# Splitting the scaled input of a three-pass float32 kernel straight from x, with x loaded in four transfers on ScalarE's queue

## The chip, the cores and the metric

The kernel runs on one core of a Trainium2 chip. The metric is the device time of one execution in microseconds (us), lower is better. The time before is the median of three runs.

## The reference, cut to what matters

Two blocks run one after the other on 256 tokens of width 1024. The first has two layers of: a gated feed-forward net of width 2816, a mixer (sliding-window attention beside a short convolution), and a second feed-forward net. Each of the six begins with an RMS norm, and a seventh norm ends the block. The second block adds 16 meta tokens and does latent attention and 2-D neighbourhood attention once.

```python
def rms_norm(x, gain):
    xf = x.astype(jnp.float32)
    inv = lax.rsqrt(jnp.mean(xf * xf, axis=-1, keepdims=True) + NORM_EPS)
    return (xf * inv).astype(x.dtype) * gain

def swiglu(h, w_gate, w_up, w_down):
    return (jax.nn.silu(h @ w_gate) * (h @ w_up)) @ w_down
...
    for l in range(DEPTH):
        x = x + 0.5 * swiglu(rms_norm(x, ffn1_norm[l]), ffn1_wg[l], ffn1_wu[l], ffn1_wd[l])
        h = rms_norm(x, mix_norm[l])
        z = h @ w_in[l]
...
        x = x + jnp.concatenate([attn_out, conv_out], axis=-1) @ w_out[l]
        x = x + 0.5 * swiglu(rms_norm(x, ffn2_norm[l]), ffn2_wg[l], ffn2_wu[l], ffn2_wd[l])
    return rms_norm(x, final_norm)
```

## The kernel before, in words

Everything is kept feature-major: `x` is a tile of 128 partitions by 8 column tiles (k = 0 to 7) by 256 tokens. Weights come from HBM in pieces, most of them 128x1024 (512 KB: eight 128x128 tiles that make one output tile of 128 features), those of the down projections 128x1408. The pieces go through four slots (`w_raw`). SyncE issues their loads (L286); a slot is loaded again once its low part is done. ScalarE writes the high part of a piece (`w_hi`, L388, in a rounded float32 format), VectorE writes the low part (`w_lo = w_raw - w_hi`, L654), and TensorE multiplies three times per weight tile (`product`, L1043 to L1045): high by high, high by low, low by high.

The input of a matmul is split in the same way into `h_hi` and `h_lo`. For the six norms inside the layers (called q = 0 to 5 here; q = 6 is the norm that ends the first block) the factor of each token is applied after the matmul, so only the norm's weight per feature has to be applied before it. That is done per column tile k in three steps:

- `scaled` (L667, VectorE): `h32 = x * weight`, the weight being one number per partition out of `sml`;
- `high` (L418, ScalarE): `hhi = h32`, rounded;
- `low` (L673, VectorE): `hlo = h32 - hhi`.

Beside it ScalarE squares x (`square`, L400) into one of two buffers `sq`, GpSimd adds the squares of k = 0 to 6 up (`add_squares`: a copy, L331, then six adds, L334), and TensorE sums that and the square of k = 7 over the partitions (`sum_norm`, L1075 and L1077). ScalarE makes the token factors of it (`rstd`, L403 and L405).

Places where these steps stand:

- **The start** (L526 to L535 on ScalarE, L847 to L857 on VectorE): x comes in two transfers of 512 KB (four k each) at the head of SyncE's queue (L281), `sml` in one on ScalarE's queue (L383). Each engine walks over the k in turn, and three splits of weight pieces stand in between.
- **The down projections** `down` (L446 and L715): 16 pieces, two per output tile; after every second piece VectorE updates x (L729), then comes the input split of that k for the next norm.
- **`wout`** (L509 and L836): eight pieces, one per k, x updated at L839.

TensorE meets the new input in `first_pair`: it runs piece 0 over k = 0 to 6, waiting for each `h_lo`, then `sum_norm`, then piece 1 over k = 0 to 6, and only then k = 7 of both:

```python
for k in (*range(KT - 1), KT - 1):
    for o in range(2) if k == KT - 1 else (0,):
        if k == 0:
            ready(0)
        pe.wait_ge(h_lo, q * KT + k + 1)
        mm = product(bank[o][:, 0:T], o, k, *hcols(k), k == 0, k == KT - 1)
...
    if k == KT - 2:
        ready(1)
        sum_norm(q)
        for k1 in range(KT - 1):
            product(bank[1][:, 0:T], 1, k1, *hcols(k1), k1 == 0, False)
```

After the second layer q = 6 takes its sum at once (`sum_norm(6)`) and TensorE has nothing else to do there; `h_hi` and `h_lo` of q = 6 are written and not used, since that norm and the next are computed in another way (`norm`). The two layers are one hardware loop on every engine.

Of the kernel before, what the change touches and what calls it, by code (L numbers as in the profile page):

```python
# [20 lines left out]
F32 = mybir.dt.float32  # L21
# [7 lines left out]
KT = D // P  # L29
# [105 lines left out]
def build(nc, xT, metaT, w8, wd, small, mats, btab, rope, colmask, metabias, relbias, out):  # L135
    with ExitStack() as ctx:
# [73 lines left out]
        x_loaded = [sem(f"x_loaded{p}") for p in range(2)]  # L210
# [65 lines left out]
        def _(sp):  # L276
            for s in raw_full:
                sp.sem_inc(s, 16 * PRIME)
            for p in range(2):
                half = slice(p * KT // 2, (p + 1) * KT // 2)  # L280
                sp.dma_start(x[:, half, 0:T], xT[:, half]).then_inc(x_loaded[p], 16)  # L281

# [37 lines left out]
        def _(pool):  # L320
# [17 lines left out]
            pool.wait_ge(h32_done, KT)  # L338
# [41 lines left out]
        def _(act):  # L380
            for s in (*hi_ready, *silu_done, pt_done):
                act.sem_inc(s, PRIME)
            act.dma_start(sml[:], small).then_inc(g_loaded, 16)  # L383
# [23 lines left out]
            def norm(q, n=T):  # L407
# [3 lines left out]
                for k in range(KT):  # L411
                    act.wait_ge(h32_done, q * KT + k + 1)
                    act.activation(hhi[:, k * TM:k * TM + n], h32[:, k % 4, 0:n], ACT.Copy).then_inc(h_hi, 1)

            def high(q, k, slot):

                act.wait_ge(h32_done, q * KT + k + 1)
                act.activation(hhi[:, bass.ds(k * TM, T)], h32[:, slot, 0:T], ACT.Copy).then_inc(h_hi, 1)  # L418
# [27 lines left out]
            def down(name, nxt, l, q):  # L446
# [5 lines left out]
                def lap(j, last):  # L452
                    for r in range(SLOTS):
                        i = r if not last else DN - SLOTS + r
                        split_ahead(name, nxt, l, i, j, last)
                        if r % 2:
                            p, o2 = r // 2, j if not last else KT // 2 - 1
                            act.wait_ge(acc_step, q * 7 + o2 * 2 + p - 1)
                            act.wait_ge(x_ready[p], q * 4 + o2 + (PRIME - 3))
                            square(p, x[:, o2 * 2 + p, 0:T])  # L460
                            high(q, o2 * 2 + p, p)
# [50 lines left out]
            def wout(l, q):  # L512
                for o in range(KT):
# [5 lines left out]
                    else:  # L519
                        act.wait_ge(acc_step, q * 7 + o - 1)  # L520
                    square(o % 2, x[:, o, 0:T])
                    high(q, o, o % 2)
# [3 lines left out]
            act.preload_act_table_set("natural_log_exp_and_others")  # L526
            for k in range(KT):
                act.wait_ge(x_loaded[k // (KT // 2)], 16)
                if k >= 2:
                    act.wait_ge(acc_step, k - 1)  # L530
                square(k % 2, x[:, k, 0:T])
                high(0, k, k % 4)
                if k in (3, 5, 7):
                    split((k - 3) // 2, PT8, uses0(1))
# [114 lines left out]
        def _(dve):  # L649
# [957 lines left out]
```

## Time and profile before

| | before |
|---|---|
| median of three runs | 1320.96 us (1319.97 to 1323.59) |
| span of the profiled execution | 1319.6 us |
| TensorE matmuls busy | 1287.5 us, 98% |
| VectorE busy | 844.0 us, 64% |
| ScalarE busy | 662.2 us, 50% |
| GpSimd busy | 127.6 us, 10% |

The span is the profiled execution's own time as the profiler sees it; it is 1.4 us below the median of the three runs. A busy share is of the whole span; the change touches a few stretches only, so these shares say which engine sets the pace in general, and the stretches have to be read one by one.

### The profile page before, as it was taken

How to read it: one execution, taken by the hardware profiler on the slowest of the kernel's cores; microseconds unless marked ns; L12 is line 12 of the kernel's file. 1: busy time of each engine (PE TensorE's matmuls, PEld its weight loads, DVE VectorE, ACT ScalarE, POOL GpSimd, SP SyncE). 2: the span in 40 equal slices, each digit the busy share in tenths (PEclk: the TensorE clock that was granted, in tenths of full speed). 3: DMA queues.
4: the chain of work that ended last, by engine and by line, in shares of the span. 5: the costliest groups of instructions: out<-in, count | busy, mean ns of one | idle time of the engine just before them, and what ended most of it. 6: DMA issues, size and time to landing. Idle time of an engine off the chain costs nothing.

```text
span 1319.6 us, 27677 instructions
## 1 busy us (share of the span) xinstructions
PE 1287.5 (98%) x10106; PEld 1220.6 (93%) x10106; DVE 844.0 (64%) x1478; ACT 662.2 (50%) x1153; POOL 127.6 (10%) x149
## 2 busy tenths in 40 slices
PE   6999999999999999999999999999889999999998
PEld 6999999999999999999999999999878769978778
DVE  6676656777667547666558676676566645456565
ACT  5554544555555445445436464554456556434443
POOL 3000000440000000000003510000110000002210
PEclk9999999999999999999999999999989999999999
DMA  7555744345556536557444465566433204433332
GB/s 278 191 188 192 230 153 156 126 144 193 184 188 226 189 103 202 191 186 239 163 133 139 136 195 182 189 212 212 133 109 128 97 1 134 138 132 96 110 99 65
DMA packets 55689, 209.87 MB, mean 159 GB/s; under 512 B 6417, under 2 KB 8465, under 8 KB 55489
## 3 DMA queue, kind: packets, MB, share of 16 engines
q1 hardware_dynamic: 54048, 203.45, 47.0%
q0 software_dynamic: 1424, 5.42, 1.4%
q8 instruction: 43, 0.70, 0.2%
q14 instruction: 30, 0.24, 0.1%
q10 hardware_dynamic: 144, 0.06, 0.0%
HBM read 207.86 MB, written 1.05 MB: 158 GB/s over the span
## 4 chain that ended last, share of the span: by engine, by line
PE 93%; DVE 4%; issue 1%; ACT 1%; DMA 0%; DVEq 0%; ACTq 0%; SPq 0%
PE bank L1043 26%; PE bank L1044 26%; PE bank L1045 25%; PE bank L1081 2%; PE bank L1390 2%; DVE w_lo L654 1%; PE bank L1355 1%; DVE h_lo L673 1%; PE bank L1344 1%; PE bank L1353 1%; PE bank L1354 1%; PE bank L1281 1%; PE bank L1386 1%; PE bank L1283 1%; PE bank L1282 1%
## 5 line engine op out<-in xcount | busy, mean ns | idle before, releaser
L1043 PE MATMUL bank<-h_hi,w_hi 128*128 128x256 f32 (+1 forms) x1992 | 568.6, 285 | 17.6 <-DVE w_lo L654 11.8
L1044 PE MATMUL bank<-h_lo,w_hi 128*128 128x256 f32 (+1 forms) x1992 | 564.4, 283 | 0.0
L1045 PE MATMUL bank<-h_hi,w_lo 128*128 128x256 f32 (+1 forms) x1992 | 559.5, 281 | 0.0
L654 DVE TENSOR_TENSOR w_lo<-w_raw,w_hi 128x1024 fp32r<-128x1024 f32 (+1 forms) x360 | 465.5, 1295 | 81.1 <-ACT w_hi L388 79.7
L388 ACT ACTIVATE w_hi<-w_raw 128x1024 fp32r<-128x1024 f32 (+1 forms) x360 | 397.3, 1107 | 92.7 <-PE bank L1045 69.7
L1043 PEld LDWEIGHTS bank<-h_hi,w_hi 128*128 128x128 f32 x1992 | 377.7, 190 | 30.5 <-issue 26.0
L1044 PEld LDWEIGHTS bank<-h_lo,w_hi 128*128 128x128 f32 x1992 | 376.9, 189 | 0.8
L1045 PEld LDWEIGHTS bank<-h_hi,w_lo 128*128 128x128 f32 x1992 | 377.4, 189 | 0.0
L1043 PE MATMUL bank<-g_hi,w_hi 128*128 128x256 f32 x832 | 232.7, 280 | 0.4 <-DVE x_res L839 0.3
L1044 PE MATMUL bank<-g_lo,w_hi 128*128 128x256 f32 x832 | 232.3, 279 | 0.0
L1045 PE MATMUL bank<-g_hi,w_lo 128*128 128x256 f32 x832 | 232.2, 279 | 0.0
L1043 PEld LDWEIGHTS bank<-g_hi,w_hi 128*128 128x128 f32 x832 | 156.4, 188 | 1.2 <-DVE x_res L839 0.7
L1044 PEld LDWEIGHTS bank<-g_lo,w_hi 128*128 128x128 f32 x832 | 156.4, 188 | 0.0
L1045 PEld LDWEIGHTS bank<-g_hi,w_lo 128*128 128x128 f32 x832 | 156.4, 188 | 0.0
L440 ACT ACTIVATE g_hi<-gated 128x256 f32 (+1 forms) x88 | 37.0, 421 | 166.3 <-DVE gated L709 166.3
L705 DVE TENSOR_TENSOR gated<-bank,rstd 128x256 f32<-128x256 f32 x88 | 37.3, 424 | 95.7 <-PE bank L1045 95.4
L400 ACT ACTIVATE squares<-x_res 128x256 f32<-128x256 f32 (+2 forms) x64 | 26.4, 417 | 126.0 <-DVE x_res L729 101.3
L701 DVE TENSOR_TENSOR squares<-bank,rstd 128x256 f32<-128x256 f32 x88 | 37.4, 425 | 46.9 <-PE bank L1045 46.9
L436 ACT ACTIVATE silu_gate<-squares 128x256 f32<-128x256 f32 x88 | 36.8, 418 | 58.0 <-DVE squares L701 58.0
L334 POOL TENSOR_TENSOR ln_mean<-ln_mean,squares 128x256 f32<-128x256 f32 (+1 forms) x45 | 44.5, 990 | 189.1 <-ACT squares L400 188.7
L331 POOL COPY ln_mean<-squares 128x256 f32<-128x256 f32 (+1 forms) x8 | 5.3, 666 | 558.6 <-ACT squares L400 558.6
L1043 PE MATMUL bank<-y_hi,w_hi 128*128 128x256 f32 (+1 forms) x168 | 51.7, 308 | 0.5 <-DVE y_lo L901 0.5
(169 smaller groups left out, 1318.0 us busy)
## 6 DMA issues: line engine op xcount, KB each, us to landing
w_raw<-in_w SPq DMA_DIRECT2D x296, 512.0 KB, 3.3
w_raw<-in_wd SPq DMA_DIRECT2D x64, 704.0 KB, 4.1
rel_bias<-in_relbias POOLq DMA_DIRECT2D x16, 192.0 KB, 2.7
btab_sb<-in_btab POOLq DMA_DIRECT2D x1, 1536.0 KB, 9.9
x_res<-in_xT SPq DMA_DIRECT2D x2, 512.0 KB, 5.1
out_T<-x_res SPq DMA_DIRECT2D x8, 128.0 KB, 1.7
rope_sb<-in_rope POOLq DMA_DIRECT2D x1, 272.0 KB, 3.9
mats_sb<-in_mats POOLq DMA_DIRECT2D x1, 192.0 KB, 3.9
```

What stands on the lines that cost most here:

```text
L334: pool.tensor_tensor(acc[:, 0:n], acc[:, 0:n], sq[:, k % 2, 0:n], ALU.add)\
L388: act.activation(whi[:, slot, 0:cols], raw[:, slot, 0:cols], ACT.Copy).then_inc(hi_ready[slot], 1)
L400: act.activation(sq[:, p, 0:src.shape[-1]], src, ACT.Square).then_inc(sq_done[p], 1)
L436: act.activation(sg[:, p], sq[:, p, 0:T], ACT.Silu).then_inc(silu_done[p], 1)
L440: act.activation(ghi[:, f, :], g32[:, p], ACT.Copy).then_inc(g_hi[p], 1)
L654: dve.tensor_tensor(wlo[:, slot, 0:cols], raw[:, slot, 0:cols], whi[:, slot, 0:cols].bitcast(F32), ALU.subtract).then_inc(lo_ready[slot], 1)
L701: dve.tensor_tensor(sq[:, p, 0:T], bank[2 * p][:, 0:T], rs[:, 0, 0:T], ALU.mult)\
L705: dve.tensor_tensor(g32[:, p], bank[2 * p + 1][:, 0:T], rs[:, 0, 0:T], ALU.mult)\
L1043: pe.matmul(o, h, xh, start=first, stop=False)
L1044: pe.matmul(o, h, xl, start=False, stop=False)
L1045: return pe.matmul(o, lo, xh, start=False, stop=last)
L1081: pe.matmul(bank[total][:, 0:n], lhs, sq[:, p, 0:n], start=first, stop=last)\
```

## The change: what it does

Three things are changed.

1. `scaled` and its tile are gone from q = 0 to 6. `high` reads x and multiplies by the weight as the activation's scale; `low` is one `scalar_tensor_tensor` (x times weight minus `hhi`). ScalarE's `high` no longer waits for VectorE. In `down` and `wout` ScalarE now does `high` before `square`.
2. At the start the squares of odd k are made by VectorE, those of even k stay with ScalarE, and the splits of the first three weight pieces stand at other k.
3. x comes in four transfers of 256 KB (two k each) on ScalarE's queue, with `sml` between the first and the second; SyncE's queue begins with the weights. ScalarE waits for `sml` before its first square. GpSimd's loads of constants wait for the eighth `h_lo` in place of the eighth `h32`.

```diff
@@ sync
-            for p in range(2):
-                half = slice(p * KT // 2, (p + 1) * KT // 2)
-                sp.dma_start(x[:, half, 0:T], xT[:, half]).then_inc(x_loaded[p], 16)
@@ gpsimd
-            pool.wait_ge(h32_done, KT)
+            pool.wait_ge(h_lo, KT)
@@ scalar
-            act.dma_start(sml[:], small).then_inc(g_loaded, 16)
+            for p in range(KT // 2):
+                two = slice(2 * p, 2 * p + 2)
+                act.dma_start(x[:, two, 0:T], xT[:, two]).then_inc(x_loaded[p], 16)
+                if p == 0:
+                    act.dma_start(sml[:], small).then_inc(g_loaded, 16)
...
-            def high(q, k, slot):
-
-                act.wait_ge(h32_done, q * KT + k + 1)
-                act.activation(hhi[:, bass.ds(k * TM, T)], h32[:, slot, 0:T], ACT.Copy).then_inc(h_hi, 1)
+            def high(q, k):
+
+                act.activation(hhi[:, bass.ds(k * TM, T)], x[:, k, 0:T], ACT.Copy,
+                               scale=sml[:, bass.ds(q * KT + k, 1)]).then_inc(h_hi, 1)
@@ down (wout alike)
-                            act.wait_ge(acc_step, q * 7 + o2 * 2 + p - 1)
                             act.wait_ge(x_ready[p], q * 4 + o2 + (PRIME - 3))
+                            act.wait_ge(acc_step, q * 7 + o2 * 2 + p - 1)
+                            high(q, o2 * 2 + p)
                             square(p, x[:, o2 * 2 + p, 0:T])
-                            high(q, o2 * 2 + p, p)
@@ scalar, the start
+            act.wait_ge(g_loaded, 16)
             for k in range(KT):
-                act.wait_ge(x_loaded[k // (KT // 2)], 16)
-                if k >= 2:
-                    act.wait_ge(acc_step, k - 1)
-                square(k % 2, x[:, k, 0:T])
-                high(0, k, k % 4)
-                if k in (3, 5, 7):
-                    split((k - 3) // 2, PT8, uses0(1))
+                act.wait_ge(x_loaded[k // 2], 16)
+                if k % 2 == 0:
+                    if k >= 2:
+                        act.wait_ge(acc_step, k - 1)
+                    square(0, x[:, k, 0:T])
+                high(0, k)
+                if k in (2, 5, 7):
+                    split((2, 5, 7).index(k), PT8, uses0(1))
@@ vector
-            def scaled(q, k, slot):
-
-                dve.tensor_scalar(h32[:, slot, 0:T], x[:, k, 0:T], sml[:, bass.ds(q * KT + k, 1)], None, ALU.mult)\
-                   .then_inc(h32_done, 1)
-
-            def low(q, k, slot):
+            def low(q, k):
+
                 dve.wait_ge(h_hi, q * KT + k + 1)
                 h = bass.ds(k * TM, T)
-                dve.tensor_tensor(hlo[:, h], h32[:, slot, 0:T], hhi[:, h].bitcast(F32), ALU.subtract)\
-                   .then_inc(h_lo, 1)
+                dve.scalar_tensor_tensor(out=hlo[:, h], in0=x[:, k, 0:T], scalar=sml[:, bass.ds(q * KT + k, 1)],
+                                         in1=hhi[:, h].bitcast(F32), op0=ALU.mult, op1=ALU.subtract).then_inc(h_lo, 1)
@@ vector, the start
-            for k in range(KT + 1):
-                if k < KT:
-                    dve.wait_ge(x_loaded[k // (KT // 2)], 16)
-                    scaled(0, k, k % 4)
-                if k > 0:
-                    low(0, k - 1, (k - 1) % 4)
-                if k in (4, 6, 8):
-                    split((k - 4) // 2, PT8, uses0(1))
+            for k in range(KT):
+                dve.wait_ge(x_loaded[k // 2], 16)
+                if k % 2:
+                    if k >= 2:
+                        dve.wait_ge(acc_step, k - 1)
+                    dve.tensor_tensor(sq[:, 1, 0:T], x[:, k, 0:T], x[:, k, 0:T], ALU.mult).then_inc(sq_done[1], 1)
+                low(0, k)
+                if k in (3, 6, 7):
+                    split((3, 6, 7).index(k), PT8, uses0(1))
```

What the order of the instructions becomes at three places. First, ScalarE's queue at the start, before:

```order
1 L383 DMA small_sb<-in_small 128x114
2 L526 ACT_TABLE_LOAD
3 L400 ACTIVATE squares<-x_res 128x256
4 L418 ACTIVATE h_hi<-h 128x256
5 L400 ACTIVATE squares<-x_res 128x256
6 L418 ACTIVATE h_hi<-h 128x256
7 L400 ACTIVATE squares<-x_res 128x256
8 L418 ACTIVATE h_hi<-h 128x256
9 L400 ACTIVATE squares<-x_res 128x256
10 L418 ACTIVATE h_hi<-h 128x256
11 L388 ACTIVATE w_hi<-w_raw 128x1024
```

and now:

```order
1 L381 DMA x_res<-in_xT 128x2x256
2 L383 DMA small_sb<-in_small 128x114
3 L381 DMA x_res<-in_xT 128x2x256 x3
4 L526 ACT_TABLE_LOAD
5 L400 ACTIVATE squares<-x_res 128x256
6 L417 ACTIVATE h_hi<-x_res,small_sb 128x256 x2
7 L400 ACTIVATE squares<-x_res 128x256
8 L417 ACTIVATE h_hi<-x_res,small_sb 128x256
9 L388 ACTIVATE w_hi<-w_raw 128x1024
10 L417 ACTIVATE h_hi<-x_res,small_sb 128x256
```

Five transfers stand ahead of the table load in place of one, and the first weight split follows five input operations in place of eight. Second, VectorE at the start, up to the second weight split, before:

```order
1 L667 TENSOR_SCALAR h<-x_res,small_sb 128x256 x2
2 L673 TENSOR_TENSOR h_lo<-h,h_hi 128x256
3 L667 TENSOR_SCALAR h<-x_res,small_sb 128x256
4 L673 TENSOR_TENSOR h_lo<-h,h_hi 128x256
5 L667 TENSOR_SCALAR h<-x_res,small_sb 128x256
6 L673 TENSOR_TENSOR h_lo<-h,h_hi 128x256
7 L667 TENSOR_SCALAR h<-x_res,small_sb 128x256
8 L673 TENSOR_TENSOR h_lo<-h,h_hi 128x256
9 L654 TENSOR_TENSOR w_lo<-w_raw,w_hi 128x1024
```

and now:

```order
1 L671 SCALAR_TENSOR_TENSOR h_lo<-x_res,small_sb,h_hi 128x256
2 L850 TENSOR_TENSOR squares<-x_res 128x256
3 L671 SCALAR_TENSOR_TENSOR h_lo<-x_res,small_sb,h_hi 128x256 x2
4 L850 TENSOR_TENSOR squares<-x_res 128x256
5 L671 SCALAR_TENSOR_TENSOR h_lo<-x_res,small_sb,h_hi 128x256
6 L656 TENSOR_TENSOR w_lo<-w_raw,w_hi 128x1024
7 L671 SCALAR_TENSOR_TENSOR h_lo<-x_res,small_sb,h_hi 128x256
8 L850 TENSOR_TENSOR squares<-x_res 128x256
9 L671 SCALAR_TENSOR_TENSOR h_lo<-x_res,small_sb,h_hi 128x256 x2
10 L656 TENSOR_TENSOR w_lo<-w_raw,w_hi 128x1024
```

Six operations stand ahead of the first weight split in place of nine. Third, ScalarE in a down projection, before (ISA and REGISTER_ALU rows are the queue's own waits and address arithmetic):

```order
67 L388 ACTIVATE w_hi<-w_raw 128x1408
68 L458 ISA
69 L459 ISA
70 L400 ISA
71 L400 ACTIVATE squares<-x_res 128x256
72 L417 ISA
73 L418 REGISTER_ALU
74 L418 ACTIVATE h_hi<-h 128x256
```

and now:

```order
62 L388 ACTIVATE w_hi<-w_raw 128x1408
63 L458 ISA
64 L459 ISA
65 L417 ISA x2
66 L417 ACTIVATE h_hi<-x_res,small_sb 128x256
67 L400 ACTIVATE squares<-x_res 128x256
```

The two have changed places.

## Rows read from the trace of the kernel before

**Rows 1.** Page, TensorE's busy time; then whom TensorE waited for (us, times)

```profile
PE 1287.5 (98%) x10106; PEld 1220.6 (93%) x10106; DVE 844.0 (64%) x1478; ACT 662.2 (50%) x1153; POOL 127.6 (10%) x149
...
PE bank L1043 <- DVE w_lo L654: 11.8, 1, 11.8
...
PE bank L1043 <- DVE h_lo L673: 2.5, 1, 2.5
```

**Rows 2.** Timeline, start: start us, us long, engine, line, operation

```profile
1.01 0.99 SPq L281 DMA_DIRECT2D x_res<-in_xT  x2
2.63 34.35 SPq L286 DMA_DIRECT2D w_raw<-in_w  x14
...
1.22 0.40 ACTq L383 DMA_DIRECT2D small_sb<-in_small  x1
...
5.64 0.42 ACT L400 ACTIVATE squares<-x_res 128x256 f32<-128x256 f32 x1 [2.71 <-DMA x_res<-in_xT]
...
10.29 1.22 DVE L654 TENSOR_TENSOR w_lo<-w_raw,w_hi 128x1024 fp32r<-128x1024 f32 x1
...
6.92 2.87 POOL L334 TENSOR_TENSOR ln_mean<-ln_mean,squares 128x256 f32<-128x256 f32 x3 [0.32 <-ACT squares L400]
...
11.78 0.58 PE L1043 MATMUL bank<-h_hi,w_hi 128*128 128x256 f32 x1 [11.78 <-DVE w_lo L654]
...
16.50 0.59 PE L1075 MATMUL bank<-ln_mean,ones_sb 128*128 128x256 f32 x2
```

**Rows 3.** Landing times of x's two loads, then of sml's (us after issue)

```profile
DMA to landing us min/median/max: 4.6/5.1/5.5
...
DMA to landing us min/median/max: 4.1/4.1/4.1
```

**Rows 4.** Stretches of the start; last: granted clock, DMA share, GB/s

```profile
2.00:5.00 3.00, 0.00 (x0) 0.00 (x0) 0.00 (x0) 0.93 (x1) 0.00 (x0) 1.00 0.82 221
5.00:8.00 3.00, 0.00 (x0) 0.00 (x0) 2.05 (x5) 1.92 (x6) 1.42 (x3) 1.00 1.07 413
8.00:11.00 3.00, 0.00 (x0) 0.00 (x0) 2.97 (x6) 2.65 (x7) 2.00 (x3) 1.00 1.01 408
```

**Rows 5.** VectorE's operations up to 18 us by form (busy, mean ns)

```profile
L667 DVE TENSOR_SCALAR h<-x_res,small_sb 128x256 f32<-128x256 f32 x8 | 5.6, 709 | 5.7 <-DMA x_res<-in_xT 5.7
...
L673 DVE TENSOR_TENSOR h_lo<-h,h_hi 128x256 fp32r<-128x256 f32 x8 | 3.3, 416 | 0.4 <-ACT h_hi L418 0.2
```

**Rows 6.** Timeline, end of the first down projection

```profile
201.06 0.42 DVE L729 SCALAR_TENSOR_TENSOR x_res<-bank,x_res 128x256 f32<-128x256 f32 x1 [1.47 <-PE bank L1045]
201.62 0.35 DVE L667 TENSOR_SCALAR h<-x_res,small_sb 128x256 f32<-128x256 f32 x1
...
201.58 0.42 ACT L400 ACTIVATE squares<-x_res 128x256 f32<-128x256 f32 x1 [3.25 <-DVE x_res L729]
...
203.31 0.60 PE L1075 MATMUL bank<-ln_mean,ones_sb 128*128 128x256 f32 x2
```

**Rows 7.** Timeline, end of the first wout

```profile
293.74 1.61 POOL L334 TENSOR_TENSOR ln_mean<-ln_mean,squares 128x256 f32<-128x256 f32 x1 [1.22 <-ACT squares L400]
...
294.67 0.96 DVE L673 TENSOR_TENSOR h_lo<-h,h_hi 128x256 fp32r<-128x256 f32 x1
295.55 0.41 DVE L839 TENSOR_TENSOR x_res<-bank,x_res 128x256 f32<-128x256 f32 x1
...
295.34 0.28 PE L1045 MATMUL bank<-h_hi,w_lo 128*128 128x256 f32 x1
295.68 0.39 PE L1043 MATMUL bank<-h_hi,w_hi 128*128 128x256 f32 x1
```

**Rows 8.** Stretches around the jump back to the second layer, columns as Rows 4

```profile
480.40:483.40 3.00, 0.53 (x5) 0.33 (x4) 1.20 (x3) 0.83 (x2) 0.00 (x0) 1.00 0.53 180
483.40:487.10 3.70, 3.70 (x20) 3.70 (x20) 0.00 (x0) 0.00 (x0) 0.00 (x0) 0.54 0.04 9
```

**Rows 9.** Timeline, after the second layer's last down projection

```profile
951.57 0.70 PE L1077 MATMUL bank<-squares,ones_sb 128*128 128x256 f32 x2 [0.59 <-ACT squares L400]
```

More of the change, by code:

```diff
@@ L209, in build @@
         w_used = [sem(f"w_used{s}") for s in range(SLOTS)]
-        x_loaded = [sem(f"x_loaded{p}") for p in range(2)]
+        x_loaded = [sem(f"x_loaded{p}") for p in range(KT // 2)]
         g_loaded = sem("g_loaded")
@@ L411, in norm @@
                 for k in range(KT):
-                    act.wait_ge(h32_done, q * KT + k + 1)
+                    act.wait_ge(h32_done, k + 1)
                     act.activation(hhi[:, k * TM:k * TM + n], h32[:, k % 4, 0:n], ACT.Copy).then_inc(h_hi, 1)
-            def high(q, k, slot):
-                act.wait_ge(h32_done, q * KT + k + 1)
-                act.activation(hhi[:, bass.ds(k * TM, T)], h32[:, slot, 0:T], ACT.Copy).then_inc(h_hi, 1)
+            def high(q, k):
+                act.activation(hhi[:, bass.ds(k * TM, T)], x[:, k, 0:T], ACT.Copy,
+                               scale=sml[:, bass.ds(q * KT + k, 1)]).then_inc(h_hi, 1)
             def late_rstd(q):
@@ L457, in lap @@
                             p, o2 = r // 2, j if not last else KT // 2 - 1
+                            act.wait_ge(x_ready[p], q * 4 + o2 + (PRIME - 3))
                             act.wait_ge(acc_step, q * 7 + o2 * 2 + p - 1)
-                            act.wait_ge(x_ready[p], q * 4 + o2 + (PRIME - 3))
+                            high(q, o2 * 2 + p)
                             square(p, x[:, o2 * 2 + p, 0:T])
-                            high(q, o2 * 2 + p, p)
                 with act.Fori(0, DN // SLOTS - 1) as j:
@@ L520, in wout @@
                         act.wait_ge(acc_step, q * 7 + o - 1)
+                    high(q, o)
                     square(o % 2, x[:, o, 0:T])
-                    high(q, o, o % 2)
                     if o == KT - 1:
@@ L731, in lap @@
                             dve.wait_ge(x_ready[p], q * 4 + o2 + (PRIME - 3))
-                            scaled(q, o2 * 2 + p, p)
-                            low(q, o2 * 2 + p, p)
+                            low(q, o2 * 2 + p)
                 with dve.Fori(0, DN // SLOTS - 1) as j:
@@ L840, in wout @@
                     dve.wait_ge(x_ready[o % 2], q * 4 + (o // 2 + PRIME - 3))
-                    scaled(q, o, o % 2)
                     if o < KT - 1:
                         split_ahead("wout", "gu2", l, o)
-                    low(q, o, o % 2)
+                    low(q, o)
                     if o == KT - 1:
```

## The prediction

> **What bounds the kernel now.** I read the page's first lines first: TensorE's matmuls are busy 1287.5 us of a span of 1319.6, VectorE 844.0 [rows 1]. So only what TensorE waits for can change the time, and the view of waits names it: 11.8 us before the first matmul and 2.5 us at one other place are the two largest that this change comes near [rows 1]. Then I read the stretches that the change touches: the start as a timeline, the end of a down projection, the end of `wout`, the jump into the second layer, and the norm that ends the first block. Outside these TensorE is fed whatever happens, and removing 56 `scaled` operations from VectorE is worth nothing there: VectorE has a third of its time free.
>
> **The start.** The reader is to see a chain: the first half of x is issued at 1.01 us and lands 4.6 us later, ScalarE's first square is at 5.64, the first weight split's low part runs from 10.29 to 11.51, the first matmul is at 11.78 and `sum_norm` at 16.50 [rows 2, 3]. Between the last two lie 21 matmuls. The same view has them 0.21 us apart, the pace of the slow stretch in [rows 8] (20 matmuls in 3.70 us at granted clock 0.54, so near the 1.2 GHz level; over the whole kernel, mostly at 2.4 GHz, it is 1287.5 us / 10106 or 0.12 to 0.13 each, [rows 1]): 21 x 0.21 = 4.4 us, and some 0.3 us of wait. The stretch views print 1.00 there, which the spacing contradicts. What the change does here has two opposite parts.
>
> *VectorE's work.* Eight `scaled` leave. They took 5.6 us together, 709 ns each, although the same operation takes 0.35 us when GpSimd is quiet; GpSimd's adds run beside them (three in 2.87 us) [rows 2, 5, 6]. Four squares come, and eight low parts stay, now with a third operand: I take 0.42 us each, the time of the update of x, which is the same kind of operation [rows 6], bounded by 0.41 (the low part now, [rows 5]) and 0.96 (a low part that meets a GpSimd add, [rows 7]). The high parts read a scale per partition in place of a fixed one; nearest is ScalarE's square, 0.42 us [rows 2]; I cost that at nothing. So 5.6 us leave VectorE and 4 x 0.42 = 1.7 us come, at the most 4 x 0.96 = 3.8. The Trainium skill (SBUF — State Buffer, "Who interferes with whom") says that both a single-input operation in the mode that uses two ports and a two-input operation with both inputs in SBUF shut GpSimd out, or are shut out by it, for a whole instruction. By that rule the new squares and low parts meet the adds as the old ones did, and the sum would take the upper figure; the low part of 0.96 us beside an add of 1.61 us [rows 7] agrees.
>
> *x's arrival.* Before, x (1.05 MB) was ahead of the weights on one queue. Now SyncE's queue starts with weights, about 1.0 us sooner (they began at 2.63, behind two x issues of 0.99 us together, [rows 2]), and x is issued by ScalarE in 0.26 MB pieces from 1.22 us on, with `sml` second. The transfers run at 221 GB/s up to 5 us and 413 up to 8, 408 up to 11 [rows 4]: 0.66 MB moved by 5.0, 1.90 by 8.0, 3.12 by 11.0, which is x and four weight pieces. Landing comes about 0.9 us after the bytes by that count (the first half's 0.52 MB and `sml`'s 0.06 are moved by 4.7 and it lands at 5.6). If both queues get the same bytes, x's first pair is there after 0.52 MB, 4.4 + 0.9 = 5.3 us. `sml` is 128 short rows (57 KB), each of which takes turns with a 4 KB row of a weight: 1.1 MB, 6.1 + 0.9 = 7.0 us, in place of 1.22 + 4.1 = 5.3 [rows 2, 3]. The second pair: 1.63 MB, 8.2 us; the third 9.5, the fourth 10.8. ScalarE starts at 7.0 in place of 5.64, does three operations and waits for the second pair. From there: square 0.4, high 0.4, weight split 1.0 (the high half; a low half takes 1.22, [rows 2]), high 0.4, low 0.4, low half of the split 1.2: 3.8 us, first matmul at 12.1. Then 21 x 0.21 gives `sum_norm` at 16.6, if what VectorE still owes it (three low parts, two squares, one split) is ready: 5 x 0.42 + 1.2 = 3.3 us, or 5 x 0.96 + 1.2 = 6.0 if each meets an add, so by 15.4 to 18.1. Only three adds are left then, so I take it as ready. **Term: +0.1 us.** Bounds: if x is not held up at all (5.3 for `sml`, 6.5 for the second pair) the first matmul is at 10.3 and the term is -1.5; if the queues take turns row by row (x's rows are 1 KB, the weights' 4 KB), x's first pair needs 1.31 MB, `sml` 1.89, the second pair 2.68: 10.8 us, first matmul 14.6, term +2.5.
>
> The third split is needed only when pieces 0 and 1 are done, some 3 us after `sum_norm`; it stays hidden. GpSimd's loads of constants now wait for the last low part, about 1 us later than for the last `scaled`; they are used by the mixer near 218 us, and cost nothing.
>
> **Down projections to the next norm** (q = 1, 3, 4). After the last piece come x_res at 201.06, square at 201.58, scaled at 201.62; then high, low, and TensorE takes `sum_norm` at 203.31 [rows 6]. TensorE runs piece 0 meanwhile (k = 0 to 6, 21 x 0.12 = 2.5 us) and needs the last square only after it, k = 7 later still. The square now ends 0.42 later, at 202.4: still 0.9 us early. **Term: 0**, hidden by piece 0.
>
> **wout** (twice). The last but one low part is held to 295.63 by GpSimd's add, and TensorE steps from 295.34 to 295.68 in place of 0.12: 0.2 us of wait [rows 7]. Without `scaled` VectorE is 0.35 us earlier; the add moves 0.4 later with its square and may meet the low part again. x_res at 295.55 stood behind that low part, so it moves up as well and the last square does not come late. I take -0.25 each, between 0 and -0.5. **Term: -0.5.**
>
> **The norm that ends the first block** (q = 6). Here nothing hides the swap. TensorE's second sum matmul is at 951.57 and waits for ScalarE's square [rows 9], which now stands behind a high part that nobody uses: 0.42 us later. VectorE waits for that chain too. **Term: +0.4**, bounds 0.3 and 0.5.
>
> Sum: +0.1 + 0 - 0.5 + 0.4 = 0.0. The profiled execution would stay at 1319.6, and the median, which is 1.4 above it, at **1321.0 us**.
>
> **Rivals.**
>
> *Late x with a cold TensorE (slower).* x's rows take turns with the longer rows of the weights. The Trainium skill (DMA: Bandwidth & Descriptors, "Issuing engines are not separate DMA queues") has transfers of different engines run on the same 16 DMA engines and interleave, so a second issuing engine buys issue time alone; by it this change can lose and not gain at the start. No row here has x beside weights, so the trace cannot say. In this kernel it is the +2.5 above in place of +0.1, 1323.4 us: 18 in 100. It passes 0.3% when TensorE's matmuls, now started late and fed in bursts, stay at the lower clock through piece 1: 27 matmuls x 0.09 us = 2.4 more, 1325.8 us. It decides from a second pair that lands after about 10.5 us. 9 in 100.
>
> *x is not held up.* Small pairs land as early as before, and VectorE's lighter load shows: the start's term goes from +0.1 to -1.5, 1319.4 us. For it speaks that `sml` landed in 4.1 us beside x before [rows 3]. 22 in 100.
>
> *The second wait of TensorE shrinks too (faster).* 2.5 us are put down to a low part [rows 1], at the jump into the second layer; after it 20 matmuls run at 0.54 [rows 8]. If it is a real wait, the chain x_res, scaled, high, low loses 0.4 us, and the slow stretch may go: 16 x 0.09 = 1.5. With 1.6 more at the start and 0.5 more in `wout` (the ends of their bounds) it is 1321.0 - 4.0 = 1317.0. Against it: the code asks there for the first low part of that norm only, done many us before, so the gap is more likely the jump itself. 6 in 100.
>
> The forecast itself, start near even: 45 in 100.
>
> **How the numbers follow.** About 0.3%, 4.0 us, is what a measurement here can tell from no change; the three runs alone spread over 3.6. Same: 45 + 22 + 18 = 85 in 100; faster 6; slower 9. The range takes in 1319.4 and 1323.4 and a run's scatter of 1 us on each side: 1318.4 to 1324.4, which leaves out most of the two outer cases.
>
> **What would show it.** Right: first matmul near 12, first square near 7, TensorE's second sum matmul of q = 6 0.4 us after where it would be, the gap at the jump 2.5 to 2.8 us, `scaled` gone and TensorE's busy time unchanged. Wrong: a first matmul before 11 or after 13; squares or low parts on VectorE of 0.8 us in the mean; a waits view with a new entry of over 1 us; a slow stretch of TensorE's clock in another place or number.

## The result, and the profile after

The changed kernel takes **1324.01 us** (median of 8 runs, 1322.4 to 1325.89) against 1321.13 us for the kernel before (8 runs on the same chip): ratio 1.0021, 95% interval 1.0011 to 1.0031. Timed again later it was 1323.91 us against 1321.41, ratio 1.0019 (1.0009 to 1.0028). That is 2.5 to 2.9 us slower: inside the predicted range of 1318.4 to 1324.4, by 0.4 us, and 0.2%, so "same" by the bound of 0.3%. The predicted time is 3 us too low all the same, and the cause is the one that was priced as a rival. Of all executions behind the times below one, in the second timing of experiment 7, took 2524.8 us for a reason that is not known; the ratios leave it out.

The profiled execution has a span of 1321.4 us (before: 1319.6). The busy line of the page and the view of waits, TensorE (for whom, us in total, times, longest):

```profile
PE 1284.9 (97%) x10106; PEld 1219.6 (92%) x10106; DVE 827.4 (63%) x1426; ACT 660.0 (50%) x1149; POOL 119.2 (9%) x149
...
PE bank L1040 <- DVE w_lo L656: 16.4, 1, 16.4
...
PE bank L1040 <- DVE h_lo L671: 2.2, 1, 2.2
PE bank L1074 <- ACT squares L400: 1.1, 1, 1.1
```

Against [rows 1] the wait before the first matmul is 16.4 us, not 11.8; the one at the jump into the second layer is 2.2, not 2.5; and the third, after the first block's last down projection, has grown from the 0.59 of [rows 9] to 1.1. VectorE's 16.6 us of less work stand in the busy line and not in the time.

The start of the changed kernel as a timeline (start us, us long, engine, line, operation, idle before and releaser in brackets), to be held against [rows 2]:

```profile
1.59 2.44 SPq L282 DMA_DIRECT2D w_raw<-in_w  x4
...
1.22 0.44 ACTq L381 DMA_DIRECT2D x_res<-in_xT  x1
1.69 0.49 ACTq L383 DMA_DIRECT2D small_sb<-in_small  x1
2.21 1.65 ACTq L381 DMA_DIRECT2D x_res<-in_xT  x3
...
7.82 0.42 ACT L400 ACTIVATE squares<-x_res 128x256 f32<-128x256 f32 x1 [2.66 <-DMA small_sb<-in_small]
8.14 0.89 ACT L417 ACTIVATE h_hi<-x_res,small_sb 128x256 fp32r<-128x256 f32 x2
11.54 0.42 ACT L400 ACTIVATE squares<-x_res 128x256 f32<-128x256 f32 x1 [2.50 <-DMA x_res<-in_xT]
...
14.38 1.75 DVE L656 TENSOR_TENSOR w_lo<-w_raw,w_hi 128x1024 fp32r<-128x1024 f32 x1
...
16.39 0.57 PE L1040 MATMUL bank<-h_hi,w_hi 128*128 128x256 f32 x1 [16.39 <-DVE w_lo L656]
...
21.02 1.05 PE L1072 MATMUL bank<-ln_mean,ones_sb 128*128 128x256 f32 x2
```

ScalarE stands still twice: to 7.82 for `sml`, and to 11.54 for the second pair of x. From there the chain is as the prediction drew it (square, high, split, low, low half of the split), and the first matmul follows 4.85 us later. The landing of x's four transfers (us after issue) says the same; in [rows 3] the two halves took 4.6 and 5.5:

```profile
DMA to landing us min/median/max: 5.1/9.8/10.4
```

The end of `wout`, VectorE and GpSimd, against [rows 7]:

```profile
293.06 0.41 DVE L836 TENSOR_TENSOR x_res<-bank,x_res 128x256 f32<-128x256 f32 x1
293.59 1.23 DVE L656 TENSOR_TENSOR w_lo<-w_raw,w_hi 128x1024 fp32r<-128x1024 f32 x1
294.74 0.97 DVE L671 SCALAR_TENSOR_TENSOR h_lo<-x_res,small_sb,h_hi 128x256 fp32r<-128x256 f32 x1
295.62 0.41 DVE L836 TENSOR_TENSOR x_res<-bank,x_res 128x256 f32<-128x256 f32 x1
...
294.57 0.85 POOL L330 TENSOR_TENSOR ln_mean<-ln_mean,squares 128x256 f32<-128x256 f32 x1 [1.72 <-ACT squares L400]
```

The weight split that stood beside the add before, to be held against the second of these lines:

```profile
293.53 1.22 DVE L654 TENSOR_TENSOR w_lo<-w_raw,w_hi 128x1024 fp32r<-128x1024 f32 x1
```

x is updated every 2.48 to 2.57 us in five steps of seven here; before, it was every 2.83 to 2.85 in five of seven (the others 2.53 and 3.21), with the update at 295.55 hard behind the low part of [rows 7]. There VectorE set the pace, and a step has become shorter by 0.3 us, about the 0.35 of one `scaled` [rows 6]. TensorE waited for it, 0.2 us each at two places (287.27 and 295.34) and 0.1 us each behind the second of them and behind the sum. Now VectorE keeps up. The low part still takes 0.97, the add 0.85 in place of 1.61. The add ends 0.60 us after the weight split in both (295.35 after 294.75; 295.42 after 294.82); it is shorter here because it starts later beside that split.

The norm that ends the first block, TensorE, against [rows 9]:

```profile
951.40 0.59 PE L1072 MATMUL bank<-ln_mean,ones_sb 128*128 128x256 f32 x2
953.11 0.70 PE L1074 MATMUL bank<-squares,ones_sb 128*128 128x256 f32 x2 [1.11 <-ACT squares L400]
```

The second sum matmul comes 1.71 us after the first; before it was 1.18 (951.57 after one at 950.39).

**Where the 1.8 us between the two profiled spans are.** Differences between the times of the same matmul in the two timelines, stretch by stretch (after minus before):

| stretch | us |
|---|---|
| to the first sum matmul (16.50, now 21.02) | +4.52 |
| first feed-forward net of layer 0 | +0.53 |
| mixer and `wout`, layer 0 | -0.51 |
| second net of layer 0 | -1.20 |
| jump into the second layer and its slow matmuls | -0.31 |
| first net of layer 1 | 0.00 |
| mixer and `wout`, layer 1 | -0.84 |
| second net of layer 1 | -1.18 |
| from the first block's last sum to the end | +0.83, of it +0.53 by the norm |

Two of these were foreseen nowhere: -1.20 and -1.18, in stages where TensorE waits for nothing. Stretches of 80 us in the second net of layer 0 (columns as in [rows 4]: length, TensorE busy with its matmuls, ...), before and then after:

```profile
320.00:400.00 80.00, 80.00 (x681) 80.00 (x681) 54.82 (x86) 39.36 (x58) 0.00 (x0) 1.00 0.57 184
```

```profile
320.00:400.00 80.00, 80.00 (x688) 80.00 (x687) 54.81 (x85) 39.88 (x57) 0.00 (x0) 1.00 0.55 188
```

681 matmuls against 688, always busy, at the same granted clock; their starts are 0.1178 and 0.1167 us apart. Whether the change did that was a question for the runs below.

### The profile page after: what moved, and what is told of

Read it like the earlier page. It is cut to its first block, busy times and chain, and to the rows that moved or that the text cites. A ratio compares the mean times of both kernels' runs of the same rounds, so it can differ in the third digit from the quotient of the medians.

```text
span 1321.4 us, 27583 instructions
## 1 busy us (share of the span) xinstructions
PE 1284.9 (97%) x10106; PEld 1219.6 (92%) x10106; DVE 827.4 (63%) x1426; ACT 660.0 (50%) x1149; POOL 119.2 (9%) x149
## 4 chain that ended last, share of the span: by engine, by line
PE 96%; ACT 1%; issue 1%; DVE 1%; DMA 1%; ACTq 0%; DVEq 0%
PE bank L1040 27%; PE bank L1041 27%; PE bank L1042 26%; PE bank L1078 2%; PE bank L1387 2%; PE bank L1352 1%; PE bank L1341 1%; PE bank L1350 1%; PE bank L1351 1%; PE bank L1278 1%; PE bank L1383 1%; PE bank L1280 1%; PE bank L1279 1%; DMA x_res<-in_xT 1%; PE bank L1382 1%
## 5 line engine op out<-in xcount | busy, mean ns | idle before, releaser
L1040 PE MATMUL bank<-h_hi,w_hi 128*128 128x256 f32 (+1 forms) x1992 | 568.5, 285 | 21.7 <-DVE w_lo L656 16.4
L417 ACT ACTIVATE h_hi<-x_res,small_sb 128x256 fp32r<-128x256 f32 (+1 forms) x56 | 28.2, 508 | 122.3 <-DVE x_res L727 107.6
L671 DVE SCALAR_TENSOR_TENSOR h_lo<-x_res,small_sb,h_hi 128x256 fp32r<-128x256 f32 (+1 forms) x56 | 33.9, 607 | 45.3 <-ACT h_hi L417 45.3
L330 POOL TENSOR_TENSOR ln_mean<-ln_mean,squares 128x256 f32<-128x256 f32 (+1 forms) x45 | 37.2, 827 | 192.0 <-ACT squares L400 188.1
```

Of the source, the lines that this page charges most:

```text
L330: pool.tensor_tensor(acc[:, 0:n], acc[:, 0:n], sq[:, k % 2, 0:n], ALU.add)\
L417: act.activation(hhi[:, bass.ds(k * TM, T)], x[:, k, 0:T], ACT.Copy, scale=sml[:, bass.ds(q * KT + k, 1)]).then_inc(h_hi, 1)
L671: dve.scalar_tensor_tensor(out=hlo[:, h], in0=x[:, k, 0:T], scalar=sml[:, bass.ds(q * KT + k, 1)], in1=hhi[:, h].bitcast(F32), op0=ALU.mul ...
L1040: pe.matmul(o, h, xh, start=first, stop=False)
```

## The experiments

Three theories stood against each other. Theory A: the start is late because rows of x take turns with rows of the weights. Theory B: it is late because of the new arithmetic. Theory C: ScalarE's queue is slow by itself.

**1. The queue alone.** The kernel before, with x and `sml` issued as in the change:

```diff
@@ sync, before
-            for p in range(2):
-                half = slice(p * KT // 2, (p + 1) * KT // 2)
-                sp.dma_start(x[:, half, 0:T], xT[:, half]).then_inc(x_loaded[p], 16)
@@ scalar
-            act.dma_start(sml[:], small).then_inc(g_loaded, 16)
+            for p in range(KT // 2):
+                two = slice(2 * p, 2 * p + 2)
+                act.dma_start(x[:, two, 0:T], xT[:, two]).then_inc(x_loaded[p], 16)
+                if p == 0:
+                    act.dma_start(sml[:], small).then_inc(g_loaded, 16)
```

> The kernel before with x in four transfers on ScalarE's queue and `sml` second there; the arithmetic is the old one. Theory A (x's 1 KB rows and the weights' 4 KB rows take turns, so x and `sml` are late): first square near 8 us, second pair landed near 11.5, first matmul near 16 in place of 11.8, nothing gained later, so the whole 4 to 5 us stay in the time: 1325 to 1326 us, ratio 1.0035. Theory B (the late start of the changed kernel comes from its arithmetic: squares on VectorE, a wait between the pairs): first matmul near 12, time as before, 1321.

Measured: 1325.47 us, ratio 1.0024 (1.0009 to 1.0039). In its timeline:

```profile
7.76 0.62 DVE L668 TENSOR_SCALAR h<-x_res,small_sb 128x256 f32<-128x256 f32 x2 [7.76 <-DMA small_sb<-in_small]
...
11.49 0.42 ACT L401 ACTIVATE squares<-x_res 128x256 f32<-128x256 f32 x1 [2.32 <-DMA x_res<-in_xT]
...
15.84 0.58 PE L1044 MATMUL bank<-h_hi,w_hi 128*128 128x256 f32 x1 [15.84 <-DVE w_lo L655]
```

The same `sml` at 7.8, the same second pair at 11.5 and a first matmul at 15.8, with the old arithmetic. Two things were missed: the first square came at 6.26, since the old code does not wait for `sml` there, and the ratio was 1.0024 where 1.0035 had been expected. B falls.

**2. The arithmetic alone.** The changed kernel, x back on SyncE's queue:

```diff
@@ sync, after
+            for p in range(2):
+                half = slice(p * KT // 2, (p + 1) * KT // 2)
+                sp.dma_start(x[:, half, 0:T], xT[:, half]).then_inc(x_loaded[p], 16)
@@ scalar
-            for p in range(KT // 2):
...
+            act.dma_start(sml[:], small).then_inc(g_loaded, 16)
```

> The changed kernel with x back in two halves at the head of SyncE's queue and `sml` alone on ScalarE's. Theory A: first square at 5.6 us as before, first matmul between 10.5 and 11.8, first sum matmul up to 1 us sooner than before; with what `wout` gave in the changed kernel's trace the time is 1.5 to 3 us below before: 1318 to 1319.5, ratio 0.998 to 0.999. Theory B: first matmul near 16 still, time near 1324.

Measured: 1319.96 us, ratio 0.9992 (0.9982 to 1.0002). First square 5.51, but first matmul 12.42, later than the 11.78 of before; first sum matmul 17.03, later by 0.5 where a gain of up to 1 was expected. The gain at the start is a miss, and the time lies 0.5 us above the range expected, with an interval that takes in no change. Its rows show why:

```profile
8.11 1.06 ACT L387 ACTIVATE w_hi<-w_raw 128x1024 fp32r<-128x1024 f32 x1 [0.67 <-DMA w_raw<-in_w]
...
8.47 0.94 DVE L849 TENSOR_TENSOR squares<-x_res 128x256 f32<-128x256 f32 x1
9.60 0.90 DVE L670 SCALAR_TENSOR_TENSOR h_lo<-x_res,small_sb,h_hi 128x256 fp32r<-128x256 f32 x1 [0.18 <-ACT h_hi L416]
10.42 1.74 DVE L655 TENSOR_TENSOR w_lo<-w_raw,w_hi 128x1024 fp32r<-128x1024 f32 x1
```

The eight `scaled` are gone, yet squares and low parts take up to 0.9 us where they meet an add of GpSimd, and the low half of the split takes 1.74 in place of the 1.22 of [rows 2].

**3. The weights wait for x**, so that x moves alone on ScalarE's queue:

```diff
@@ sync, after
+            for p in range(KT // 2):
+                sp.wait_ge(x_loaded[p], 16)
             def load(src, cols, slot, count):
```

> The changed kernel, x on ScalarE's queue, but SyncE waits for all four pairs of x before its first weight load, so x moves alone. Theory A: the first pair lands near 4 us, `sml` near 5 and the last pair near 6; the first weight piece lands near 9.5 and its split ends near 11.5 to 12: first matmul 12 to 13, time 1320 to 1321, some 3 us below the changed kernel. If it is ScalarE's queue itself that is slow (Theory C: the issuing queue, not the neighbour), the first square stays at 7.5 or later and the first matmul goes to 15 or more.

Measured: 1324.34 us, ratio 1.0018 (1.0009 to 1.0027).

```profile
8.30 2.30 SPq L284 DMA_DIRECT2D w_raw<-in_w  x4
...
DMA to landing us min/median/max: 3.3/4.2/4.4
...
5.02 0.42 ACT L402 ACTIVATE squares<-x_res 128x256 f32<-128x256 f32 x1
...
11.65 1.06 ACT L390 ACTIVATE w_hi<-w_raw 128x1024 fp32r<-128x1024 f32 x1 [4.56 <-DMA w_raw<-in_w]
...
15.56 0.58 PE L1042 MATMUL bank<-h_hi,w_hi 128*128 128x256 f32 x1 [15.56 <-DVE w_lo L658]
```

Without weights beside it the same four transfers on the same queue land 3.3 to 4.4 us after issue, not 5.1 to 10.4, and the first square is at 5.0, not 7.8: C falls. The whole time was a miss: SyncE issues its first weight only at 8.30, where 6 or so had been expected, and the gate is now the weight. Waiting trades one lateness for the other.

**4. Four transfers on SyncE's queue:**

```diff
@@ sync, after
+            for p in range(KT // 2):
+                two = slice(2 * p, 2 * p + 2)
+                sp.dma_start(x[:, two, 0:T], xT[:, two]).then_inc(x_loaded[p], 16)
@@ scalar
...
+            act.dma_start(sml[:], small).then_inc(g_loaded, 16)
```

> The changed kernel with x in four transfers at the head of SyncE's queue, ahead of the weights, and `sml` alone on ScalarE's. Theory A: rows of one queue do not take turns with those behind them, so the first pair lands near 4.5 us and the last near 7; the four issues cost about 0.5 us each, so the weights start near 3.5; first matmul 10.5 to 11.8, time 1318 to 1319.5, the same as or up to 0.5 us below the two halves. Theory B: first matmul near 16, time near 1324.

Measured: 1321.8 us, ratio 0.9998 (0.9989 to 1.0007), 2.3 us above the range expected. Landing takes 3.4 to 4.7 us after issue and the first square is at 4.59, but the weights start at 3.63, `w_hi` at 8.81 and the first matmul is at 12.72; the first sum matmul comes at 16.59, the 16.50 of before. Cutting x in four gained nothing in either queue; taking it off SyncE's queue lost 4.4 us.

**5. Short rows for the weights.** If turns go by row, shorter weight rows must help x:

```diff
@@ sync, after
-                sp.dma_start(raw[:, slot, 0:cols], src).then_inc(raw_full[slot], 16)
+                if cols == PT8:
+                    src = src.rearrange("p (c n) -> p c n", n=256)
+                sp.dma_start(raw_rows(slot, cols), src).then_inc(raw_full[slot], 16)
```

> The changed kernel with every 0.5 MB weight piece written as rows of 1 KB in place of 4 KB (same bytes, same queues, same issues; the raw piece lies in four parts with gaps, and the splits read it so). If the two queues take turns by row, x's 1 KB rows now get half of the DMA engines' time in place of a fifth: `sml` near 6 to 6.5 us, the second pair near 7.5 to 8.5 in place of 11.5, the fourth before 11, while the first weight piece comes later, near 9 to 10. If they share by bytes, or if ScalarE's queue is slow by itself, the second pair stays at 11 or later. Whole time: no forecast, since short rows make all later loads slower too.

```profile
6.27 0.42 ACT L411 ACTIVATE squares<-x_res 128x256 f32<-128x256 f32 x1 [1.08 <-DMA small_sb<-in_small]
...
7.94 0.42 ACT L411 ACTIVATE squares<-x_res 128x256 f32<-128x256 f32 x1 [0.45 <-DMA x_res<-in_xT]
...
12.54 0.58 PE L1051 MATMUL bank<-h_hi,w_hi 128*128 128x256 f32 x1 [12.54 <-DVE w_lo L667]
```

`sml` 6.3, second pair 7.9, first matmul 12.5 in place of 16.4, with the same bytes, queues and issues. The first sum matmul is at 16.56, where it was at 16.50 before and 21.02 in the changed kernel: the whole loss is gone. The last pair landed 8.5 us after its issue, at 11.7, where before 11 had been expected, and the first weight split starts at 8.66, sooner than the 9 to 10 expected for its piece. Its one run took 1320.99 us. The trace's DMA records, counted by queue, row size and the time of their start, show the turns themselves:

```
us          changed kernel: x rows / weight rows     short weight rows: x rows / weight rows
8 to 9               87 (1 KB) / 80 (4 KB)                    173 (1 KB) / 206 (1 KB)
9 to 10              82        / 80                           188        / 185
```

One row of each in turn, and in the changed kernel the counts stay between 18 and 23 of each in every quarter of a microsecond from 7.75 to 10.25. At 412 GB/s in all (9 to 10 us), x moves 0.08 MB per us, a fifth: its 256 rows per pair take 3.1 us. This is the row-by-row rival, shown. The Trainium skill (DMA: Bandwidth & Descriptors, "Issuing engines are not separate DMA queues") has transfers of several issuing engines interleave and gain only issue time; the trace agrees, 4.4 us lost and none gained. The same page ("Queues, rings and completion order") has an engine drain some 9 to 17 descriptors of one queue before it turns to the next; equal counts in each quarter microsecond, a little over one row of each kind per DMA engine, do not look like that, and the measurement decides. The records do not say which engine moved a row, so this is read from the sums: nine 4 KB rows at the 0.159 us that each takes here are 1.4 us, and sixteen engines that drained so many at a time would have to be evenly out of step to give such counts.

**6. `sml` first:**

```diff
@@ scalar, after
+            act.dma_start(sml[:], small).then_inc(g_loaded, 16)
             for p in range(KT // 2):
                 two = slice(2 * p, 2 * p + 2)
                 act.dma_start(x[:, two, 0:T], xT[:, two]).then_inc(x_loaded[p], 16)
-                if p == 0:
-                    act.dma_start(sml[:], small).then_inc(g_loaded, 16)
```

> The changed kernel with `sml` issued ahead of x's four transfers on ScalarE's queue. If turns by row decide, `sml` is there near 5 us and the first square moves from 7.8 to 5.7 to 6.5, but the second pair still has 256 rows of each kind behind it and comes at 10.5 to 11.5: the first matmul stays within 0.5 us of the changed kernel's 16.2 to 16.4. If it is `sml` that holds up the start, the first matmul comes 1.5 to 2 us sooner.

```profile
7.24 0.42 ACT L399 ACTIVATE squares<-x_res 128x256 f32<-128x256 f32 x1 [1.97 <-DMA x_res<-in_xT]
...
10.38 0.42 ACT L399 ACTIVATE squares<-x_res 128x256 f32<-128x256 f32 x1 [1.93 <-DMA x_res<-in_xT]
...
15.24 0.57 PE L1039 MATMUL bank<-h_hi,w_hi 128*128 128x256 f32 x1 [15.24 <-DVE w_lo L655]
```

`sml` now lands 1.8 us after issue, before the weights move, and saves its turns: the second pair is 1.2 us sooner, the first matmul 1.0 to 1.15. That is more than the 0.5 allowed and less than the 1.5 of the other reading. The first square is at 7.24, later than the 5.7 to 6.5 expected, and waits for x's first pair now. Most of the loss is x's own rows. One run: 1324.0 us.

**7. The old start with the new arithmetic elsewhere**, and the square ahead of the high part:

```diff
@@ scalar, down (and so in wout), after
+                            square(p, x[:, o2 * 2 + p, 0:T])
                             high(q, o2 * 2 + p)
-                            square(p, x[:, o2 * 2 + p, 0:T])
@@ start on sync, scalar, vector and gpsimd: as in the kernel before
```

> The kernel before at the start (scaled copies, x in halves on SyncE's queue, old order of operations there), the new arithmetic in the down projections and `wout` alone, and there the square ahead of the high part as before. If the profiles read so far are right: first matmul 11.8 as before, first sum matmul 16.5, 0.5 to 0.8 us gained in each `wout`, 0 to 0.3 at the jump, nothing lost at the norm that ends the first block (second sum matmul 1.18 us after the first, not 1.71): 1.2 to 1.9 us below before, 1319.3 to 1320, ratio 0.9986 to 0.9991. If the order of square and high is not what costs there, the distance stays 1.7 us.

Measured: **1318.82 us**, ratio **0.9982** (0.9973 to 0.9991), a little more gain than expected. First matmul 11.70, first sum 16.57. At the norm that ends the first block:

```profile
948.25 0.59 PE L1084 MATMUL bank<-ln_mean,ones_sb 128*128 128x256 f32 x2
949.46 0.70 PE L1086 MATMUL bank<-squares,ones_sb 128*128 128x256 f32 x2 [0.61 <-ACT squares L399]
```

1.21 us apart with the new arithmetic, where it was 1.18 before and 1.71 in the changed kernel, so it was the order of square and high that cost 0.5 there. It was run again:

> The kernel with the old start and the new arithmetic in `wout` and the down projections once more, beside the one above on the same chip. Expected 1318.5 to 1320, ratio 0.998 to 0.999. In its profile: the last norm of the first block 1.2 us between its two sum matmuls, each stretch from a norm through `wout` 92.0 to 92.3 us where the kernel before has 92.8 to 92.9, and some pattern of 1.1 us steps in the gate and up stages that need not be that of the first profile.

Measured: 1319.5 us against 1322.57, ratio 0.9979 (0.9969 to 0.9988), the same norm again 1.21 us. Its `wout` answers a question that the changed kernel left open:

```profile
288.58 1.22 DVE L658 TENSOR_TENSOR w_lo<-w_raw,w_hi 128x1024 fp32r<-128x1024 f32 x1
...
289.07 1.34 POOL L333 TENSOR_TENSOR ln_mean<-ln_mean,squares 128x256 f32<-128x256 f32 x1 [1.22 <-ACT squares L399]
```

With `scaled` gone but the square first again, the add starts sooner, takes 1.34 us, and again ends 0.6 us after the split. The stretch is as short as in the changed kernel (92.15 us, table below), so the shorter add is not what gained the time; the absence of `scaled`, which both kernels share, is.

**8. Both kernels once more**, unchanged, for second profiles:

> The kernel before once more, for a second profile. TensorE's matmuls in the four gate and up stages went at 0.1178 or 0.1167 us each, some 1.2 us of difference in a stage; three of the four were at 0.1178 in the first profile. If the pace is a matter of the run, another pattern comes for the same program; if the program sets it, the same three stages are slow again.

> The changed kernel once more, for a second profile and more timed runs. In its first profile one of the four gate and up stages was at 0.1178 us per matmul, against three in the profile of before. If that is a matter of the run, the pattern changes and a run with more slow stages has a span up to 3.6 us above 1321.4; if the program sets it, the same pattern and 1321.4 within 0.5. Timed: 1323.5 to 1325, ratio 1.002 to 1.003. First matmul at 16.4 and second sum matmul of the last norm 1.7 us after the first in either case.

The span of before was 1318.6 us (1319.6 first), that of the changed kernel 1323.2 (1321.4 first). The same 80 us of the second net of layer 0, changed kernel, and then the first net of layer 0 (40 to 120 us) in the kernel before, which had 682 matmuls in its first profile:

```profile
320.00:400.00 80.00, 80.00 (x681) 80.00 (x681) 54.31 (x84) 39.28 (x57) 0.00 (x0) 1.00 0.55 185
```

```profile
40.00:120.00 80.00, 80.00 (x688) 80.00 (x687) 55.45 (x87) 40.19 (x59) 0.00 (x0) 1.00 0.55 185
```

The same program goes at either pace. The starts of matmuls in the timelines give this table (us). A slow net takes 186.8 in place of 185.7 (first net of a layer) or 184.3 in place of 183.2 (second). "Jump and slow matmuls" runs from the last matmul before the gap at the jump to the first sum matmul of the second layer. The column q = 6 is the distance of the two sum matmuls at the end of the first block, and the last one the time from the first of them to the kernel's last matmul:

| profile | first matmul | first sum | mixer and `wout`, layers 0, 1 | slow nets of 4 | jump and slow matmuls | q = 6 | rest |
|---|---|---|---|---|---|---|---|
| before | 11.78 | 16.50 | 92.83, 92.90 | 3 | 6.85 | 1.18 | 366.3 |
| before, again | 11.61 | 16.60 | 92.89, 92.82 | 3 | 4.78 | 1.18 | 367.4 |
| queue alone | 15.84 | 20.90 | 92.84, 92.83 | 4 | 4.95 | 1.19 | 366.9 |
| after | 16.39 | 21.02 | 92.32, 92.06 | 1 | 6.54 | 1.71 | 367.2 |
| after, again | 16.23 | 20.86 | 92.17, 92.12 | 4 | 4.77 | 1.70 | 368.1 |
| arithmetic alone | 12.42 | 17.03 | 92.04, 92.13 | 3 | 5.24 | 1.71 | 366.9 |
| old start | 11.70 | 16.57 | 92.28, 92.17 | 4 | 5.01 | 1.21 | 367.5 |
| old start, again | 11.68 | 16.71 | 92.15, 92.17 | 3 | 5.21 | 1.21 | 366.1 |
| experiment 9 | 10.88 | 15.78 | 92.34, 92.23 | 2 | 6.34 | 1.20 | 367.3 |

The columns of the start, of `wout` and of q = 6 follow the code. The slow nets, the jump and the last stretch do not: they differ as much between two profiles of one program. Where the jump's column has 6.3 to 6.9, 18 to 20 matmuls after the gap start 0.21 us apart (the slow stretch of [rows 8]); where it has 4.8 to 5.2, only 4 do.

**9. A try at a better kernel:** x in halves on SyncE's queue, all first squares on ScalarE, VectorE's first two splits one tile sooner, none of the scaled copies:

```diff
@@ scalar, start, arithmetic alone
-                if k % 2 == 0:
-                    if k >= 2:
-                        act.wait_ge(acc_step, k - 1)
-                    square(0, x[:, k, 0:T])
+                if k >= 2:
+                    act.wait_ge(acc_step, k - 1)
+                square(k % 2, x[:, k, 0:T])
@@ vector, start
-                if k % 2:
...
-                    dve.tensor_tensor(sq[:, 1, 0:T], x[:, k, 0:T], x[:, k, 0:T], ALU.mult).then_inc(sq_done[1], 1)
-                if k in (3, 6, 7):
+                if k in (2, 5, 7):
@@ down and wout: the square ahead of the high part
```

> A try at a better kernel: x in halves at the head of SyncE's queue, the new arithmetic everywhere, but all eight first squares on ScalarE as before (none on VectorE), the first split one tile sooner, and the square ahead of the high part in `wout` and the down projections. VectorE's start holds eight low parts and three splits alone. Expected from rows of the runs before: first matmul 10.5 to 11.5, first sum matmul 15.3 to 16.3, `wout` -0.7 each, norm at the end of the first block as before: 2 to 3.5 us below before, ratio 0.9974 to 0.9985. If the start is set by ScalarE (eight squares, eight high parts of 0.49 us and three splits of 1.04), the first sum matmul stays at 16.5 and the time equals that of the kernel with the old start, 1318.8.

Measured: 1318.85 us against 1322.57, ratio **0.9974** (0.9963 to 0.9986).

```profile
8.30 1.06 ACT L387 ACTIVATE w_hi<-w_raw 128x1024 fp32r<-128x1024 f32 x1 [0.41 <-DMA w_raw<-in_w]
...
9.39 1.23 DVE L654 TENSOR_TENSOR w_lo<-w_raw,w_hi 128x1024 fp32r<-128x1024 f32 x1 [0.57 <-ACT w_hi L387]
...
10.88 0.57 PE L1034 MATMUL bank<-h_hi,w_hi 128*128 128x256 f32 x1 [10.88 <-DVE w_lo L654]
...
15.78 0.59 PE L1066 MATMUL bank<-ln_mean,ones_sb 128*128 128x256 f32 x2
```

The split follows the weight's landing at once, the first matmul is 0.9 us and the first sum 0.7 us sooner than before. It beats both kernels. It had the same runs of before as the second run of the old start, whose interval overlaps its own (0.9969 to 0.9988), so that it is the better of those two is seen at the start and not in the time.

## Why the prediction came out as it did

The time lay in the range by a sum whose largest term was wrong, and that is partly luck: `wout` gained 0.9 us more than its term and hid so much of the start's miss of 4.3.

- **The start, +0.1 forecast, +4.4 measured** (mean of two profiles each: 20.94 against 16.55 at the first sum). The step that failed is "if both queues get the same bytes". They get the same number of rows. The prediction had taken `sml`'s rows one by one in turn with the weights' and x's rows by bytes, in the same sum. The rival with row-by-row turns had the right rule, and its 10.8 us for the second pair was near the 11.5 seen, but its price of +2.5 was still too low: 0.7 us too early for the pair, and from the pair to the first matmul 4.85 us where the sum had 3.8. Of the second, 0.5 is the low half of the split at 1.75, costed at 1.2. The "at the most" figure for the small operations was applied to squares and low parts, but not to the split. Its sum 14.6 + 4.4 left no wait at the first sum, and there was none before it.
- **Cold TensorE.** The forecast put it at +2.4 from a second pair later than 10.5 us. The pair was later, but the slow matmuls were 20 in place of 17 (at about 0.21 us each, from 16.8 us on), and the first net was 0.05 and 0.5 us longer than the slow 186.81 of before; the 0.5 are the sum matmuls, 0.42 us apart in place of 0.21 in the first of the two profiles. Piece 1 ran at 0.12 us. That rival fell.
- **`scaled` leaves VectorE.** That this is worth nothing at the start was half right for the wrong reason: 5.6 us left and squares, low parts and splits grew by what they met, so the start with the new arithmetic alone was 0.5 us later. With the squares kept on ScalarE, and VectorE's first two splits one tile sooner, the same removal gave 0.7 us; which of the two did it was not tried.
- **Down projections, 0.** Held: the piece behind which the square hides was enough in every profile (203.31 moved by 5.05 with the start and the slow matmuls, no wait before it).
- **`wout`, -0.25 each.** The mechanism held, the size was off: 92.85 us before (mean of six stretches in three profiles) against 92.17 (four stretches of the changed kernel), -0.7 each. I looked at the last wait alone ([rows 7]). VectorE had been the pace-setter over most of the stage, at 2.84 us a step with `scaled` and 2.5 without, and TensorE had waited at 287.27 as well and after the sum.
- **q = 6, +0.4.** Held: +0.52, undone by turning square and high round.
- **The jump.** Put down to the jump itself and not to the low part: gaps of 2.75 and 2.23 us in two profiles of before, 2.43 and 2.21 in two of the changed kernel. It differs by the run, and so does the slow stretch behind it (20 and 4 matmuls in the two of before, 18 and 4 in the two of the changed kernel), which that rival had hoped would go. That rival fell.
- **The sum.** +4.4 - 1.4 + 0.5 + 0.3 = +3.8 us from rows, against +2.9 and +2.5 timed (1.2 to 4.1 by the intervals). The old start is -1.4 by rows and was timed at -2.4 and -2.8 (-1.2 to -4.1). Both lie about 1 us below the rows. Whether that is chance or a gain in the second block, where profiles of one program differ by 1 us and more, stays open.

Of the signs named before, "first matmul after 13" and an entry of over 1 us in the waits (the q = 6 one, 1.1) came true and told of the right failure.

## What to carry to other kernels

When a small, urgent load shares the DMA engines with bulk loads of another queue, count rows, not bytes: with rows of 1 KB against 4 KB it gets a fifth of the bandwidth, and a bulk queue that starts 1 us sooner can cost 4. Put the urgent load at the head of the same queue; rows of equal length helped too (experiment 5), and longer rows for the urgent load were not tried. Taking work off an engine that is not the bottleneck paid here in the one stage where that engine set the pace; look for it stage by stage, by the spacing of its own operations, before the share of the whole span says it cannot matter.

## What the runs showed that I had not expected

- The gate and up part of every feed-forward net of this kernel runs at one of two paces, 0.1178 or 0.1167 us per matmul, at the same granted clock and with TensorE never idle (681 or 682 against 688 in 80 us). The same net of the same program is at either in different executions; each slow one costs 1.1 us, and there are four. What picks it is not known. It is a good part of the 3 to 4 us by which runs of one kernel differ, and it made the first pair of profiles look closer (1.8 us) than the second (4.6).
- VectorE's low part with the scale folded in takes 0.48 us where the plain one took 0.42, and 0.97 beside an add of GpSimd where the plain one took 0.96. The add beside it took 0.85 in place of 1.61, and 1.34 with the square first: how long it takes is set by how early it starts beside the weight split, whose end it outlasted by 0.6 us in all three. The Trainium skill (SBUF — State Buffer, "Who interferes with whom") has a VectorE instruction with two inputs in SBUF contend with a GpSimd instruction that reads SBUF; the low parts and the weight splits agree.
